# One kernel, three blocks: the stick-breaking attention's output laid out by tokens instead of by channels before its head norm

## The reference, cut to what matters

```
z = einsum(q, k) / sqrt(64)                      # 8 heads of 64, queries in blocks of 128
mask = k_pos < q_pos                             # strictly causal
log_not = where(mask, log_sigmoid(-z), 0)
suffix = cumsum(log_not, reverse=True) - log_not
weights = where(mask, exp(log_sigmoid(z) + suffix), 0)
o = einsum(weights, v)
...
o = o * rsqrt(mean(o * o, axis=-1) + 1e-6)       # over the 64 channels of a head
o = o.reshape(S, 512) * attn_out_g
pooled = multiscale_pool(u, w_pool, pool_scale)
mixed = concatenate([o, pooled]) @ w_out
```

## Time and profile before

| | |
|---|---|
| time, median of 3 runs | 5290.67 us (5284.02 to 5294.39) |
| profiled execution, time | 5284.02 us |
| its span, first to last instruction | 5282.3 us |
| busy share of the span | TensorE 87%, VectorE 36%, ScalarE 23%, GpSimd 18% |
| the attention's rounds and their end | 3976 to 4255 us of the span |

### The profile page before, as it was taken

One profiled execution on the slowest core, in us unless ns is written; L12 is line 12 of the kernel. 1 busy time (PEld: TensorE's weight loads), 2 busy tenths in 40 slices (PEclk: granted clock), 3 DMA queues, 4 the chain that ended last, 5 costly groups with the idle time before them and its releaser, 6 DMA issues.

```text
span 5282.3 us, 46530 instructions
## 1 busy us (share of the span) xinstructions
PE 4585.9 (87%) x19720; PEld 3106.4 (59%) x19720; DVE 1893.1 (36%) x3103; ACT 1217.7 (23%) x2191; POOL 934.6 (18%) x520
## 2 busy tenths in 40 slices
PE   8888988888799989646898988899998898999988
PEld 4766757566588873334343444444445576888877
DVE  2435344352223131884512223101215723333343
ACT  3222122221122220112212333200015512112233
POOL 1101001011112441920000000100000014333353
PEclk9999888989899989855998998999998788999999
DMA  2000000000211120000001000112000002111110
GB/s 83 14 2 24 1 25 1 13 1 28 73 41 33 48 80 16 18 26 0 16 24 40 24 16 24 39 35 80 32 32 1 1 24 72 48 48 48 48 56 33
DMA packets 125313, 167.87 MB, mean 32 GB/s; under 512 B 7472, under 2 KB 90288, under 8 KB 125104
## 3 DMA queue, kind: packets, MB, share of 16 engines
q1 hardware_dynamic: 125104, 164.88, 9.5%
HBM read 156.48 MB, written 8.39 MB: 31 GB/s over the span
## 4 chain that ended last, share of the span: by engine, by line
PE 44%; DVE 4%; ACT 2%; DMA 1%; issue 1%; POOL 1%; POOLq 0%; ACTq 0%; DVEq 0%
PE bank L450 18%; PE bank L461 6%; PE bank L483 5%; PE bank L485 5%; PE bank L484 5%; PE bank L472 2%; PE bank L1019 1%; PE bank L1034 1%; DMA W<-w_in 1%; PE bank L927 1%; PE bank L941 1%; DVE BIG L2516 0%; DVE BIG L2527 0%; PE bank L819 0%; DVE XT L2519 0%
## 5 line engine op out<-in xcount | busy, mean ns | idle before, releaser
L450 PE MATMUL bank<-XT,W 128*128 128x512 f32 x3168 | 1425.1, 607 | 101.2 <-DMA W<-w_in 69.0
L450 PEld LDWEIGHTS bank<-XT,W 128*128 128x128 f32 x3168 | 610.0, 195 | 860.0 <-issue 832.9
L483 PE MATMUL bank<-W_r,BIG_r 128*128 128x256 f32 (+1 forms) x1024 | 345.8, 338 | 7.1 <-DVE MIX_r L2224 4.5
L485 PE MATMUL bank<-W_r,BIG_r 128*128 128x256 f32 (+1 forms) x1024 | 344.3, 336 | 0.0
L483 PE MATMUL bank<-XT_r,W_r 128*128 128x512 f32 x768 | 300.2, 391 | 8.2 <-POOL BIG_r L2890 8.2
L484 PE MATMUL bank<-BIG_r,W_r 128*128 128x512 f32 x768 | 299.8, 390 | 0.0
L461 PE MATMUL bank<-W,MIX 128*128 128x256 f32 (+1 forms) x896 | 258.7, 444 | 16.2 <-DMA W<-w_out 10.0
L472 PE MATMUL bank<-ident,H 128*128 128x128 f32 x616 | 125.7, 340 | 167.2 <-ACT H L1525 77.9
L2890 POOL TENSOR_TENSOR BIG_r<-MIX,W_r 128x2048 fp32r<-128x2048 f32 x36 | 165.4, 4596 | 329.8 <-ACT W_r L1686 329.8
L461 PEld LDWEIGHTS bank<-W,MIX 128*128 128x128 f32 x896 | 168.9, 192 | 92.8 <-issue 77.6
L1148 ACT ACTIVATE BIG<-bank 128x512 f32<-128x512 f32 (+3 forms) x193 | 105.4, 547 | 483.4 <-PE bank L450 153.9
(11 more groups left out here) (399 smaller groups left out, 7756.3 us busy)
## 6 DMA issues: line engine op xcount, KB each, us to landing
W<-w_in SPq DMA_DIRECT2D x17, 2048.0 KB, 8.1
MIX<-w_up SPq DMA_DIRECT2D x16, 1024.0 KB, 5.5
MIX<-w_down SPq DMA_DIRECT2D x16, 1024.0 KB, 4.9
W<-w_in_e SPq DMA_DIRECT2D x26, 512.0 KB, 6.6
W<-w_in_o SPq DMA_DIRECT2D x12, 1024.0 KB, 5.1
H<-x SPq DMA_DIRECT2D x16, 512.0 KB, 7.5
W<-w_out_e SPq DMA_DIRECT2D x4, 1024.0 KB, 5.3
W<-w_out_o SPq DMA_DIRECT2D x4, 1024.0 KB, 5.2
```

The source lines that it names most:

```text
L450: mm = E.matmul(b[:, :], wv[:, k, c0:c0 + P], src[:, k, half * HALF:(half + 1) * HALF], start=k == 0, stop=k == kt - 1)
L483: E.matmul(b[:, 0:n], lh, rh, start=k == ks[0], stop=False)
L485: mm = E.matmul(b[:, 0:n], ll, rh, start=False, stop=k == ks[-1])
```

## The change

The product with V gets its operands swapped: the transposed weights are stationary (128 keys x 128 queries) and V moves (64 channels). The output then lies by tokens, 128 queries on the partitions and all 512 channels along a row. The square is as before. In round `k + 5` VectorE sums the squares of each head along the row, into 8 columns, and scales them, and ScalarE takes the root of 8 columns. In round `k + 6` VectorE takes the reciprocal of 8 columns and multiplies the output by it, broadcast over the 64 channels of a head, into `O_S`. In round `k + 7` TensorE transposes `O_S` in four pieces into a bank of the transposes' ring. In round `k + 8` VectorE multiplies that bank by the gain into `MIX`.

```diff
--- before.py
+++ after.py
@@ -1031,16 +1031,12 @@
                     for a0 in range(0, i + 1, 4):
                         pe.wait_ge(*done("ev", "stick", "p_tr", i, h, a0))
                     for j in range(i + 1):
-                        mm = E.matmul(b_out[64 * (h % 2):64 * (h % 2) + 64, h // 2 * P:(h // 2 + 1) * P],
-                                      VN_S[:, j, h * 64:(h + 1) * 64], PT_S[k % 2][:, j * P:(j + 1) * P], start=j == 0,
-                                      stop=j == i)
+                        mm = E.matmul(b_out[:, h * 64:(h + 1) * 64], PT_S[k % 2][:, j * P:(j + 1) * P],
+                                      VN_S[:, j, h * 64:(h + 1) * 64], start=j == 0, stop=j == i)
                     mm.then_inc(*stick.pe.mark("stick", "pv", k))
-                for i in stick_tiles(r, 5):
-                    b = for_stick_t.open("stick", "sums", i)
-                    pe.wait_ge(*for_stick_t.free("stick", "sums", i))
-                    pe.wait_ge(*done("stick", "o_sq", i))
-                    E.matmul(b[:, :], head_ones[:, :], SQ_S, start=True, stop=True).then_inc(
-                        *stick.pe.mark("stick", "sums", i))
+                for i in stick_tiles(r, 7):
+                    pe_transposes(stick, for_stick_t, ("o_tr", i), [O_S[i % 2][:, j * P:(j + 1) * P] for j in range(4)],
+                                  done("ev", "stick", "o", i))
 
         def pe_outp():
             after(pe, stick)
@@ -1675,9 +1671,9 @@
                     act.wait_ge(*done("stick", "pv", r - 4))
                     S.activation(SQ_S, for_stick_o.bank("stick", "o", i)[:, :], ACT.Square).then_inc(
                         *stick.act.mark("stick", "o_sq", i))
-                for i in stick_tiles(r, 6):
-                    act.wait_ge(*done("ev", "stick", "sums", i))
-                    S.activation(O_S[i % 2], O_S[i % 2], ACT.Sqrt).then_inc(*stick.act.mark("stick", "o_sd", i))
+                for i in stick_tiles(r, 5):
+                    act.wait_ge(*done("stick", "o_var", i))
+                    S.activation(ST_S, ST_S, ACT.Sqrt).then_inc(*stick.act.mark("stick", "o_sd", i))
 
         def act_split_high(st, k, loaded, *waits):
             act.wait_ge(*loaded)
@@ -2518,19 +2514,27 @@
                     dve.wait_ge(*stick.dve.last())
                     V.tensor_tensor(A_S[k % 3][:, 0:n], A_S[k % 3][:, 0:n], C_[:, 1:n + 1], ALU.mult).then_inc(
                         *stick.dve.mark("stick", "p", i, h))
+                for i in stick_tiles(r, 5):
+                    dve.wait_ge(*done("stick", "o_sq", i))
+                    V.tensor_reduce(ST_S, SQ_S.rearrange("p (h n) -> p h n", h=8), AX.X, ALU.add).then_inc(
+                        *stick.dve.mark())
+                    dve.wait_ge(*stick.dve.last())
+                    V.tensor_scalar(ST_S, ST_S, 1.0 / 64, 1e-6, ALU.mult, ALU.add).then_inc(
+                        *stick.dve.mark("stick", "o_var", i))
                 for i in stick_tiles(r, 6):
-                    dve.wait_ge(*done("stick", "sums", i))
-                    V.tensor_scalar(O_S[i % 2], for_stick_t.bank("stick", "sums", i)[:, :], 1.0 / 64, 1e-6, ALU.mult,
-                                    ALU.add).then_inc(*stick.dve.mark("ev", "stick", "sums", i))
-                for i in stick_tiles(r, 7):
+                    O3 = O_S[i % 2].rearrange("p (h n) -> p h n", h=8)
                     dve.wait_ge(*done("stick", "o_sd", i))
-                    V.reciprocal(O_S[i % 2], O_S[i % 2]).then_inc(*stick.dve.mark())
+                    V.reciprocal(ST_S, ST_S).then_inc(*stick.dve.mark())
                     dve.wait_ge(*stick.dve.last())
-                    for ct in range(4):
-                        V.scalar_tensor_tensor(MIX[:, ct, i * P:(i + 1) * P],
-                                               for_stick_o.bank("stick", "o", i)[:, ct * P:(ct + 1) * P],
-                                               col("attn_out_g_3", ct), O_S[i % 2][:, ct * P:(ct + 1) * P], ALU.mult,
-                                               ALU.mult).then_inc(*stick.dve.mark("ev", "stick", "o", i))
+                    V.tensor_tensor(O3, for_stick_o.bank("stick", "o", i)[:, :].rearrange("p (h n) -> p h n", h=8),
+                                    ST_S.unsqueeze(2).to_broadcast([P, 8, 64]), ALU.mult).then_inc(
+                                        *stick.dve.mark("ev", "stick", "o", i))
+                for i in stick_tiles(r, 8):
+                    dve.wait_ge(*done("stick", "o_tr", i))
+                    V.tensor_tensor(MIX[:, 0:4, i * P:(i + 1) * P],
+                                    for_stick_t.bank("stick", "o_tr", i)[:, :].rearrange("p (c n) -> p c n", c=4),
+                                    cols("attn_out_g_3", 0, 4, P), ALU.mult).then_inc(
+                                        *stick.dve.mark("ev", "stick", "o_tr", i))
 
         def dve_outp():
             after(dve, stick)
```

## The result

The changed kernel takes 5365.18 us (median of 4 runs, 5359.14 to 5373.11) beside 5288.86 us for the kernel before: a ratio of 1.0145, 95% interval 1.0128 to 1.0163. It is slower by 76 us; the forecast was 5265 us, and the second rival, the clock that doesn't come back, had given about 5370.

The account below looks back on a forecast made before the run. TensorE was taken to bound undisturbed rounds, bank waits and VectorE's norm chain the tile boundaries. Gain 50.8 less 9 for additions and 16 for the clock gave 26 us: 5258, or 5265 beside the median; range 5240 to 5288.

Parts of the forecast that it names:

- the second rival: Stick-breaking stage: clock never returns after the start, items 4 to 47 cost 125 us more against 42 gained; about 5370, chance 0.07.
- The clock: Stage's start and after each of three bank waits: one round more on the low clock, 16 us in all.
- Product with V at 0: Product with V: swapped operands keep matmuls about 0.112 us apart, weight loading cancelling the narrower moving side; 0 us.
- Gross gain 50.8, additions 9: Tile boundaries and stage end: removing the old norm chain saves 50.8 us; new VectorE, ScalarE and TensorE work adds 9.
- The bank wait moves and stays: After tiles 7, 6 and 5: next item's transposes still wait some 3.4 us; 5.5 us per boundary with slow products stays.
- Boundary after tile 7: Six rounds after tile 7: 11.7 us above undisturbed rounds, 5.5 of it staying as bank wait, 6.2 to be had.
- The end: Last item's norm chain before the output projection: 4.2 us instead of 8.2, saving 4.0.
- The late sigmoids: Round 5 of a boundary: ScalarE's table fetches make next sigmoids about 1.2 us late, delaying transposes; 2.3 us in all.
- the long reciprocal was mostly hidden: Rival at tile boundaries: VectorE's reciprocal cost little, the low clock came without it; some 10 us gained, 5281, chance 0.08.
- the new product takes half the time: Rival for the product with V: only the 64 moving columns count; 25 us more saved, 5240, chance 0.05.

Follow-up runs that it names:

- own bank: Changed kernel with the transposes of O in the output's own bank instead of the transposes' ring: 5353.51 us; same edit on the wide operand's kernel: 5223.63 us.
- the wide operand: Changed kernel with the product with V moving 128 columns (this head's and the next's, surplus overwritten) instead of 64: 5248.81 us, ratio 0.992.
- the old product: Changed kernel with the old operands of the product with V (64 stationary, 128 moving columns), new norm chain kept: 5251.15 us, ratio 0.9926.
- thin from tile 6 on, with and without the ring: Changed kernel, product with V moving 128 columns in tile 7, 64 afterwards: 5318.78 us with the transposes' ring, 5234.97 us with O's transposes in the output's bank.

## Why the prediction was wrong

The step that failed is the one under "The clock": one round more on the low clock at the stage's start and after each of three bank waits, 16 us. The clock did not come back at all after the start, also not on items 4 to 47, the 44 of the 64 that the prediction counts as able to run at the full clock, and the swap alone is enough for it. In place of 16 us more, TensorE was on 1.2 GHz for all but about 6 of the stage's 351 us, where before it was for some 117 of 279. The prediction had this as its second rival, at 125 us against a gain of 42, "about 5370"; it gave it 0.07. That the number fits is in part luck. The swap alone costs 86 us, not 125; the kernel before is on the low clock for part of these items too (0.88 over 4036 to 4080 us, 0.85 over 4080 to 4115). And taking out the old norm chain gains 10 us on the low clock, not 42. Both terms are too large, and the excess cancels.

What the runs showed in place of the step is a lock, not a surcharge. On the low clock 16 matmuls of the thin product span 3.5 us, and TensorE, which with its own bank does not idle for 298 us on end, does not get the full clock back in any round. That the narrow moving operand does it is shown by the wide operand and by the old product, each of which brings the clock back. Why the chip holds it back is not shown.

The argument against that rival was that the clock comes back each time today while scores and transposes are untouched. That was read from a kernel whose third matmul group moved 128 columns. No row of before shows the thin product on the low clock without gaps, and the prediction took a middle value between 0 and never. In the changed kernel and the three others that have the thin product and no ones-product (own bank; thin from tile 6 on, with and without the ring), a clock that had fallen under the thin product never came back within the stage. The window attention was the nearest row, and it pointed the right way, although with TensorE busy for 52 of its 112 us it could not decide.

The Trainium skill (TensorE: Matmul & The Clock Gate, Part 1: The HAM clock gate) says that the throttled state is the default and activity releases it. The stops that end in 0.50 agree, and so does the return with the wide operand. The changed kernel measures something that this sentence does not lead one to expect: with TensorE 100% busy in the profile over 4036 to 4080 us, the clock stays at 0.50.

The other steps, against the wide operand's kernel, in which the clock comes back after stops:

- *Product with V at 0.* Right. Thin, wide and old form span 1.67, 1.73 and 1.74 us for 14 at the full clock.
- *Gross gain 50.8, additions 9, so 42 us with the clock left as it was.* Measured 5289.89 - 5248.81 = 41.1. The clock was not left as it was, though: 0.86 over the stage against 0.79 before. The total is confirmed by this, and of the terms only the two below.
- *The bank wait moves and stays, 3.4 us and 5.5 with the slow product.* Right after tile 7: 3.46 us for the gain product, and in the wide kernel's chain the round from 4051.66 to 4061.30 takes 9.64 us beside 4046.69 - 4036.87 = 9.82 before. But the waits are worth more than was worked out: with the own bank 25 us go, against 3 x 5.5.
- *Boundary after tile 7: 6.2 to be had, less 0.44 and 0.3.* Six rounds take 31.3 us in the wide kernel (4038.19 to 4069.45) against 36.8: 5.5.
- *The end.* 4.2 us were worked out from the square to the projection. Changed kernel, last tile:

```profile
4333.73 0.69 DVE L2519 TENSOR_REDUCE STAT<-BIG 128x8 f32<-128x512 f32 x1 [2.31 <-ACT BIG L1672]
4334.45 0.17 DVE L2522 TENSOR_SCALAR STAT<-STAT 128x8 f32<-128x8 f32 x1
4335.00 0.21 ACT L1676 ACTIVATE STAT<-STAT 128x8 f32<-128x8 f32 x1
4335.25 0.20 DVE L2527 RECIPROCAL STAT<-STAT 128x8 f32<-128x8 f32 x1 [0.63 <-ACT STAT L1676]
4335.48 0.69 DVE L2529 TENSOR_TENSOR BIG<-bank,STAT 128x512 f32<-128x512 f32 x1
...
4336.23 1.11 PE L472 MATMUL bank<-ident,BIG 128*128 128x128 f32 x4 [3.17 <-DVE BIG L2529]
4337.38 0.69 DVE L2534 TENSOR_TENSOR MIX<-bank,PAR 128x512 f32<-128x512 f32 x1 [1.21 <-PE bank L472]
```

From 4333.71 to 4338.28 that is 4.6 us against 8.2. Each duration is as priced, and the 0.4 more than worked out is the root's wait for its table, which ScalarE fetches from 4333.71 to 4334.99, when the square is done; the variance is ready at 4334.62.

- *The late sigmoids.* In the wide kernel after tile 7 they start 1.7 us behind their mask, where 0.3 is usual: 1.4 us late, 1.2 was worked out. The transposes wait 0.25 us for the copy behind them there, but 0.53 after tile 6, 1.09 after tile 5 and up to 1.20 in the short rounds: more than the tenths that the prediction allowed. Together these stops are 5.6 us against 3.6 before, so 2 us more, where 2.3 was worked out.
- *Two other rivals.* That the long reciprocal was mostly hidden is out on the full clock, by the 41 us; on the low clock it is so, by the 10 us. That the new product takes half the time is out by the spans above.

## What to carry to other kernels

Before the moving operand of a matmul is made narrower, look at where TensorE stops, and at whether the narrower work brings the full clock back afterwards; if that isn't known, the price of the change runs from nothing to a doubling of the stage's TensorE time. A busy share near 100% with the granted clock at 0.50 in the same stretch is the sign, and widening the moving operand with columns that nobody reads can be the cure when the wider product takes hardly longer, as here (1.73 us for 14 against 1.67). Where a small step such as a row-wise norm borrows a bank from a ring that the main loop needs, give it the bank that it has just read.

## What was not expected of the hardware

The granted clock depends on what went before. The same instructions in the same order, thin product in tiles 6 to 0, run tile 6 at 1.00 in one kernel and at 0.50 in another, 271 matmuls or 148 in the same 44 us, by the product of tile 7 before them, which moved 128 columns or 64 behind the same stops at the start. One stop of 3.45 us then sets off a loss of most of 84 us in a stage of 220 (5318.78 against 5234.97). And throwing away work made TensorE faster: 128 moving columns of which half are overwritten took 116 us less than the 64 that are needed.
